# Seven block products for eight in 14 slabs of the down projections of a two-block transformer kernel

## The reference, cut to what matters

```python
def swiglu(x, w_gate, w_up, w_down):          # D_MODEL 1024, D_FF 2816
    return (jax.nn.silu(x @ w_gate) * (x @ w_up)) @ w_down

x = layer_norm(alpha * x + 0.5 * swiglu(...), ln_g[l, 0], ln_b[l, 0])        # first block
h = h + 0.5 * _swiglu(_rmsnorm(h, ffn_norm[layer, 0]), w_gate_up, w_down)    # second block
```

## Time and profile before

| what | value |
|---|---|
| median of 3 runs | 1599.74 us (1599.69 to 1599.82) |
| span of the profiled execution, first to last instruction | 1597.9 us |
| the profiled execution's own time | not listed apart from its span; the median of the runs is 1.8 us above the span |
| TensorE busy | 1591.1 us, 8788 matmuls |
| TensorE weight loads busy | 1369.5 us |
| VectorE busy | 1031.5 us, 1228 instructions |
| ScalarE busy | 801.4 us, 1092 instructions |
| DMA | 291.2 MB, 182 GB/s, 55.2% of the 16 engines |
| granted TensorE clock | 1.000 of full over the whole span |

### The profile page before, as it was taken

How to read it: one execution, slowest core, us unless ns; L and a number is a source line. 1 busy time by engine, 2 the same in 40 slices (tenths; PEclk the granted TensorE clock), 3 DMA queues, 4 the chain that set the end, 5 groups by cost and what they waited for, 6 DMA issues and landing times.

```text
span 1597.9 us, 21193 instructions
## 1 busy us (share of the span) xinstructions
PE 1591.1 (100%) x8788; PEld 1369.5 (86%) x8788; DVE 1031.5 (65%) x1228; ACT 801.4 (50%) x1092; POOL 35.5 (2%) x53
## 2 busy tenths in 40 slices
PE   9999999999999999999999999999999999999999
PEld 7888898878888888888899888889888888988887
DVE  6665656798766647665557666557766557766662
ACT  5555254775455525554344555446555436545550
POOL 0000000000000000000000000001000011000000
PEclk9999999999999999999999999999999999999999
DMA  9565574445567546665465655558565551056551
GB/s 308 187 218 184 171 260 154 141 139 181 170 196 231 199 163 199 194 200 186 157 224 176 194 185 203 197 171 254 175 189 199 187 198 56 28 174 192 187 186 77
DMA packets 226591, 291.21 MB, mean 182 GB/s; under 512 B 10628, under 2 KB 203840, under 8 KB 226368
## 3 DMA queue, kind: packets, MB, share of 16 engines
q1 hardware_dynamic: 226224, 289.61, 55.2%
q10 hardware_dynamic: 272, 0.26, 0.0%
HBM read 288.78 MB, written 1.05 MB: 181 GB/s over the span
## 4 chain that ended last, share of the span: by engine, by line
PE 95%; DVE 3%; ACT 1%; POOL 0%; issue 0%; DVEq 0%
PE bank L2089 24%; PE bank L2094 12%; PE bank L1878 9%; PE bank L1883 9%; PE bank L1887 9%; PE bank L1966 6%; PE bank L1958 6%; PE bank L1953 6%; PE bank L1927 2%; PE bank L1934 2%; PE bank L1929 2%; PE bank L2496 1%; PE bank L1854 1%; DVE w_lo L1160 1%; PE bank L2460 1%; PE bank L2471 1%
## 5 line engine op out<-in xcount | busy, mean ns | idle before, releaser
L1160 DVE TENSOR_TENSOR w_lo<-raw,w_hi 128x2048 fp32r<-128x2048 f32 (+1 forms) x267 | 599.3, 2269 | 166.8 <-ACT w_hi L729 164.5
L729 ACT ACTIVATE w_hi<-raw 128x2048 fp32r<-128x2048 f32 (+1 forms) x266 | 504.9, 1905 | 169.0 <-DMA raw<-in_ffn_w_down_dram 93.4
L2089 PE MATMUL bank<-xT,w_hi 128*128 128x512 f32 x1664 | 397.3, 391 | 0.0
L2089 PEld LDWEIGHTS bank<-xT,w_hi 128*128 128x128 f32 x1664 | 306.2, 188 | 59.5
L2094 PEld LDWEIGHTS bank<-xT,w_lo 128*128 128x128 f32 x1664 | 213.3, 191 | 8.1
L2094 PE MATMUL bank<-xT,w_lo 128*128 128x256 f32 x1664 | 215.9, 283 | 0.0
L1107 ACT ACTIVATE silu<-bank 128x256 f32<-128x256 f32 x104 | 34.2, 381 | 215.9 <-PE bank L2094 215.9
L1883 PE MATMUL bank<-w_hi,hT_lo 128*128 128x512 f32 x528 | 134.9, 390 | 0.0
L1878 PE MATMUL bank<-w_hi,hT_hi 128*128 128x512 f32 x528 | 133.8, 389 | 0.0
L1887 PE MATMUL bank<-w_lo,hT_hi 128*128 128x512 f32 x528 | 133.7, 389 | 0.0
L1953 PE MATMUL bank<-w_hi,xT 128*128 128x512 f32 (+2 forms) x448 | 117.6, 391 | 0.0
(11 more groups left out here) (294 smaller groups left out, 1572.4 us busy)
## 6 DMA issues: line engine op xcount, KB each, us to landing
raw<-in_ffn_w_gate_up_dram SPq DMA_DIRECT2D x176, 512.0 KB, 4.8
raw<-in_ffn_w_down_dram SPq DMA_DIRECT2D x132, 512.0 KB, 4.1
raw<-in_w_in_dram SPq DMA_DIRECT2D x44, 512.0 KB, 4.9
raw<-in_ffn_w_gate_dram SPq DMA_DIRECT2D x42, 512.0 KB, 4.0
raw<-in_ffn_w_up_dram SPq DMA_DIRECT2D x42, 512.0 KB, 5.0
raw<-in_conv_w_in_dram SPq DMA_DIRECT2D x24, 512.0 KB, 4.6
raw<-in_kv_w_dram SPq DMA_DIRECT2D x12, 512.0 KB, 4.4
raw<-in_w_out_dram SPq DMA_DIRECT2D x8, 512.0 KB, 3.9
```

What stands on the lines that cost most here:

```text
L729: nc.scalar.activation(w_hi[:, slot, 0:width], raw[:, slot, 0:width], ACT.Copy).then_inc(high_ready, 1)
L1160: nc.vector.tensor_tensor(w_lo[:, slot, 0:width], raw[:, slot, 0:width], w_hi[:, slot, 0:width].bitcast(F32), ALU.subtract).then_inc(low_r ...
L2089: nc.tensor.matmul(o[:], hi[:, c, at], x, start=kh == 0 and c == 0, stop=False, skip_group_check=True)
```

## The change

Three of the 11 down slabs (d = 3, 5, 7) in stages 0, 3, 5 and 9, and two (d = 3, 5) in stage 2, 14 in all, are multiplied by Strassen's method. The 2x2 blocks of the activations are (row block c of the slab) x (token tile); those of the weights are (row block) x (column half). The order of the down slabs becomes 0, 3, 1, 5, 2, 7, 4, 6, 8, 9, 10 (in stage 2: 0, 3, 1, 5, 2, 4, 6, 7, 8, 9, 10). Such a slab takes two slots: slot k has the loaded blocks, of which three are split; slot k + 1, for which nothing is loaded, gets four sums of blocks that VectorE makes in `raw`, and they are then split as any slab. VectorE also makes four sums of activation blocks in the tile after the silu. TensorE runs 9 matmuls on slot k and 12 on slot k + 1 in place of 24; four of the seven products go to banks 0, 1, 4 and 5, which the stage's last feature tile has used, and three straight to `Y`. Behind the last such slab ScalarE copies one bank out and VectorE adds the four shared products to the residual.

```diff
+SEVEN = {0: (3, 5, 7), 2: (3, 5), 3: (3, 5, 7), 5: (3, 5, 7), 9: (3, 5, 7)}
-    first_slab = [sum(LENGTH[k] for k in phases[:n]) for n in range(len(phases) + 1)]
+    first_slab = [sum(LENGTH[k] + len(SEVEN.get(m, ())) for m, k in enumerate(phases[:n])) for n in range(len(phases) + 1)]
...
+        P1, P5, P6, P7 = bank[0], bank[5], bank[1], bank[4]
...
+        def down_order(n):
+            plain = [d for d in range(FC // 2) if d not in sevens(n)]
+            order = []
+            for d in sevens(n):
+                order += [plain.pop(0), d]
+            return order + plain
...
+            if k in BLOCKS_OF:
+                return 3 * 512
...
+            def blocks(w, c0):
+                def pieces(slot):
+                    dst = raw[:, slot, :].rearrange("p (a n) -> p a n", a=4)
+                    return [(dst[:, 0:4:3, :], w[c0 * P:(c0 + 1) * P, :].rearrange("p (a n) -> p a n", a=2)),
+                            (raw[:, slot, 512:1536], w[(c0 + 1) * P:(c0 + 2) * P, :])]
+                return pieces
...
@@ ScalarE
-                act.wait_ge(arrived[slot], 32 * (k // SLOTS + 1))
+                if k in SUMS_OF:
+                    act.wait_ge(b_sums, SUMS_OF[k] + 1)
+                else:
+                    act.wait_ge(arrived[slot], 32 * loads_to(k))
...
+                        if j - 1 in sevens(n):
+                            i = sevens(n).index(j - 1)
+                            act.wait_ge(s_made, seven_before[n] + i + 1)
+                            nc.scalar.activation(s_hi[:, i], s_raw[:, i], ACT.Copy).then_inc(s_high, 1)
...
+                    if sevens(n):
+                        split_to(first_slab[n + 1] - 2)
+                        act.wait_ge(slab_used, last_seven(n))
+                        nc.scalar.activation(silu[:].rearrange("p a b -> p (a b)"), P1[:], ACT.Copy).then_inc(p1_copied, 1)
...
@@ VectorE
+            def block_sums(k):
+                b = raw[:, k % SLOTS, :].rearrange("p (a n) -> p a n", a=4)
+                made = raw[:, (k + 1) % SLOTS, :].rearrange("p (a n) -> p a n", a=4)
+                dve.wait_ge(arrived[k % SLOTS], 32 * loads_to(k))
+                dve.wait_ge(slab_used, k + 2 - SLOTS)
+                step(nc.vector.tensor_tensor(made[:, 0:2, :], b[:, 0:3:2, :], b[:, 3:4, :].to_broadcast([P, 2, 512]), ALU.subtract))
+                step(nc.vector.tensor_tensor(made[:, 2, :], b[:, 2, :], made[:, 0, :], ALU.add))
+                nc.vector.tensor_tensor(made[:, 3, :], b[:, 1, :], made[:, 2, :], ALU.subtract).then_inc(b_sums, 1)
...
+            def shared_products(n, factor):
+                w, p1 = h[:].rearrange("p a b -> p (a b)"), silu[:].rearrange("p a b -> p (a b)")
...
+                dve.wait_ge(p1_copied, ffn_seven[n] + 1)
+                step(nc.vector.tensor_tensor(w, P6[:], p1, ALU.add))
+                onto(first, P1[:])
+                onto(second, w)
+                step(nc.vector.tensor_tensor(p1, P7[:], w, ALU.add))
+                step(onto(rest, p1.unsqueeze(1).to_broadcast([P, 2, 512])))
+                nc.vector.scalar_tensor_tensor(out=right, in0=P5[:].unsqueeze(1).to_broadcast([P, 2, 512]), scalar=-1.0 if has_ln(n) else -factor,
+                                               in1=right, op0=ALU.mult, op1=ALU.add)
...
                         nc.vector.tensor_tensor(h[:], silu[:], h[:], ALU.mult).then_inc(h_ready, 2)
+                        if j in sevens(n):
+                            token_sums(j)
...
+                        if j - 1 in sevens(n):
+                            dve.wait_ge(s_high, seven_before[n] + i + 1)
+                            nc.vector.tensor_tensor(s_lo[:, i], s_raw[:, i], s_hi[:, i].bitcast(F32), ALU.subtract).then_inc(s_ready, 1)
...
+                    def token_sums(j):
+                        s, a = s_raw[:, sevens(n).index(j)], [[h[:, c, tt * P:(tt + 1) * P] for c in range(2)] for tt in range(NT)]
+                        dve.wait_ge(h_ready, 2 * FT * f + 2 * j + 2)
+                        nc.vector.tensor_tensor(s[:, 2, :], a[0][0], a[1][0], ALU.subtract)
+                        step(nc.vector.tensor_tensor(s[:, 0, :], a[1][0], a[1][1], ALU.add))
+                        step(nc.vector.tensor_tensor(s[:, 1, :], s[:, 0, :], a[0][0], ALU.subtract))
+                        nc.vector.tensor_tensor(s[:, 3, :], a[0][1], s[:, 1, :], ALU.subtract).then_inc(s_made, 1)
...
+                    if sevens(n):
+                        split_to(first_slab[n + 1] - 2)
+                        dve.wait_ge(slab_used, last_seven(n))
+                        shared_products(n, 0.5)
...
@@ TensorE
+                    def seven_products(k, d):
...
+                        own = [(P1, tokens(0, 0), 0), (Y[0][0], tokens(1, 0), 1), (Y[0][1], combined(3), 2)]
+                        made = [(P5, combined(0), 0), (P7, combined(2), 1), (P6, combined(1), 2), (Y[1][0], tokens(1, 1), 3)]
+                        pe.wait_ge(s_ready, seven_before[n] + i + 1)
+                        if i == 0:
+                            pe.wait_ge(up_joined, joined_before[n] + FT - token_tiles(n))
+                        for slab, group in ((k, own), (k + 1, made)):
+                            hi, lo = slab_view(slab % SLOTS, 4, 512)
+                            pe.wait_ge(high_ready, slab + 1)
+                            for o, (x_hi, _), at in group:
+                                nc.tensor.matmul(o[:], x_hi, hi[:, at, :], start=i == 0 and o in (P1, P5, P6, P7), stop=False, skip_group_check=True)
+                            for o, (_, x_lo), at in group:
+                                nc.tensor.matmul(o[:], x_lo, hi[:, at, :], start=False, stop=False, skip_group_check=True)
+                            pe.wait_ge(low_ready, slab + 1)
+                            for o, (x_hi, _), at in group:
+                                ins = nc.tensor.matmul(o[:], x_hi, lo[:, at, :], start=False, stop=d == sevens(n)[-1] and o in (P1, P5, P6, P7),
+                                                       skip_group_check=True)
+                            ins.then_inc(slab_used, 1)
```

More of the change, by code:

```diff
@@ L568, in _ @@
                     gains(n)
-                    for d in range(FC // 2):
-                        load(s0 + 2 * FT + d, rows(down, 2 * d))
+                    for i, d in enumerate(down_order(n)):
+                        load(down_slab(n, i), (blocks if d in sevens(n) else rows)(down, 2 * d))
                 elif kind == MIXER:
@@ L1201, in add_output, with onto @@
                 ins.then_inc(summed, 1)
+            def shared_products(n, factor):
+                w, p1 = h[:].rearrange("p a b -> p (a b)"), silu[:].rearrange("p a b -> p (a b)")
+                first, second, rest = x_sb[:, 0, 0:512], x_sb[:, 0, 512:D], x_sb[:, 1, :].rearrange("p (a n) -> p a n", a=2)
+                right = x_sb[:].rearrange("p t (a n) -> p t a n", a=2)[:, :, 1, :]
+                def onto(x, y):
+                    if has_ln(n):
+                        return nc.vector.scalar_tensor_tensor(out=x, in0=x, scalar=ALPHA / factor, in1=y, op0=ALU.mult, op1=ALU.add)
+                    return nc.vector.scalar_tensor_tensor(out=x, in0=y, scalar=factor, in1=x, op0=ALU.mult, op1=ALU.add)
+                dve.wait_ge(p1_copied, ffn_seven[n] + 1)
[6 more added lines that the diff above has]
+                                               in1=right, op0=ALU.mult, op1=ALU.add)
             def layer_norm(n, tt, factor):
@@ L1835, in _ @@
                         tile(j)
[L1836 to L1839, removed]
+                    if sevens(n):
+                        split_to(first_slab[n + 1] - 2)
+                        dve.wait_ge(slab_used, last_seven(n))
+                        shared_products(n, 0.5)
+                    split_to(first_slab[n + 1] + 3 - tail(n))
+                    boundary(n, 0.5, first_slab[n + 1])
         @block.tensor
@@ L1875, in part @@
                     if not known:
-                        pe.wait_ge(high_ready, s0 + d + 1)
+                        pe.wait_ge(high_ready, k + 1)
                     for c, toks, at, o in each:
-                        nc.tensor.matmul(o, lhs_hi[:, 2 * d + c, toks], hi[:, c, at], start=d == 0 and c == 0, stop=False,
+                        nc.tensor.matmul(o, lhs_hi[:, 2 * d + c, toks], hi[:, c, at], start=i == 0 and c == 0, stop=False,
                                          skip_group_check=True)
-                    for i, (c, toks, at, o) in enumerate(each):
-                        if between and i == len(each) // 2:
+                    for m, (c, toks, at, o) in enumerate(each):
+                        if between and m == len(each) // 2:
                             between()
@@ L1884, in part @@
                     if not known:
-                        pe.wait_ge(low_ready, s0 + d + 1)
+                        pe.wait_ge(low_ready, k + 1)
                     for c, toks, at, o in each:
```

(7 more changed lines are left out.)

49 lines of the change are left out of this document (41 added, 8 removed).

## The result

The kernel after takes **1591.09 us** (median of 4 runs, 1590.62 to 1591.44), the kernel before 1599.78 beside it (4 runs, 1599.69 to 1599.95). The ratio is 0.9946 [0.9934, 0.9957]: 8.7 us or 0.54% faster, where 9.5 were forecast. It lies inside the predicted range, 0.9 us above the predicted time.

A forecast was written before the change was run, and what follows sets the result against it. TensorE was taken to bound the kernel, matmul by matmul. Span 1597.9 less 9.52 us for 42 matmuls, added VectorE and ScalarE work costing 0, gives 1588.4; with 1.84 around it 1590.2 us, range 1589.3 to 1594.3.

The forecast's parts named there:

- TensorE sets the time: Down projections: 42 matmuls fewer at 226.7 ns take 9.52 us off, as long as the other engines keep up.
- the rival by which a matmul is worth 184 ns: Down projections: a removed matmul saves only its weight load's time, 7.7 us in all, 1592.0 us; chance 0.02.
- the one in which 21 take as long as 24: Rival, down slabs: matmuls spaced at 259 ns in place of 227, so no gain, 1599.7 us; chance 0.06.
- Cost of the sums: VectorE, each of 14 slabs: block sums 1.23 + 0.69 + 0.69 us, 2.66 with self-waits; upper end 5.3 us.
- partial cover: Rival: first pair and stage 0's boundary each late, 1 to 5 us given back, 1591.2 to 1595 us; chance 0.14.
- the overrun of VectorE: Rival, down stage: VectorE becomes the bound, slower from about 1.5 times the operations' cost, 1635 us at double; chance 0.06.
- First pair: First two slots, stage 0: joins end near 134.7, TensorE needs them at 137.1; cover 2.4 us, cost 0.
- Boundary of stage 0: End of stage 0's down projection: `y_ready` at 181.5, room for 2.5 to 4.3 us more VectorE work, cost 0.
- What is late first: If wrong: `y_ready` finds VectorE in its splits, and the transposes of the next stage's input wait.
- the price that the prediction put on doubled sums: First pair: joins end near 137.3, TensorE waits 0.2 to 1 us in each of five stages, 1 to 5 us.
- The high end of the range: 1594.3 us: most of the partial cover, up to doubled sums at the first pair in four or five stages.
- the allowance around the span: Whole kernel: 1.84 us between the profiled span and the median of the runs, added to the span of 1588.4.

The follow-up runs named there:

- Experiment 4: The kernel after with each seven-product down slab put ahead of the plain slab instead of behind it: 1607.62 us, ratio 1.005.
- experiment 3: The kernel after with each of the three block-sum operations run twice, same results: 1597.89 us, ratio 0.9989.

## Why the prediction was right

- *TensorE sets the time, and 42 matmuls are worth 227 ns each.* Shown. 9.50 us came out of the down projections against 9.52 counted; the rival by which a matmul is worth 184 ns (7.7 us) falls, and so does the one in which 21 take as long as 24. The Trainium skill's 131 ns for a matmul of 512 columns (TensorE: Matmul & The Clock Gate, Back-to-back issue gap) is in no run here; the pair of slots goes at 226.7 ns too.
- *Cost of the sums.* 1.22, 0.69 and 0.69 us, as plain operations of the width, so neither partial cover nor the overrun of VectorE came about. VectorE has 1138 us in place of 1147: rows back to back overlap by up to 0.08 us, which the sum counted twice, and the shared products took 5.1 us (166.35 to 171.48) for 5.5.
- *First pair.* Sums end at 128.5 for 129.0 forecast, the low part of slot k + 1 at 132.8 for 133.2, the joins at 134.1 for 134.7; cover 2.9 us for 2.4. Experiment 4 shows what the cover is worth.
- *Boundary of stage 0.* `y_ready` at 181.4 for 181.5 forecast, and 0.49 us of idle left ahead of it. The small margin was right.
- *What is late first.* Half right. The boundary was named; the low part of the third pair was not, and in experiment 3 it gives 4.5 us of wait. The step counted the work from 137.5 to `y_ready` as one sum and saw 3.1 us left, but each pair has a due time of its own. In the kernel after, the low part of slot k ends 4.5 us ahead of its due time at the second pair and 5.6 at the third; when every pair gets 2.66 us more, the third has to carry three of them and is the first to fail. So the price that the prediction put on doubled sums, a wait at the first pair and 1 to 5 us in all, was wrong in its place and its size: 0.17 us there in stage 0, and 6.9 in all. The high end of the range rests on that price, and the plain cost of the sums kept it from being tested by the result.
- *The 0.9 us that are missing.* The sum left out the mixer, 0.57 of span: 0.36 of it shown, by instructions that do nothing, to come from the place of instructions in VectorE's list. The step that failed is that a stage without an edit costs nothing. The other 0.2 is at the mixer's end, and it too comes only with seven products in stage 0. There ScalarE's copy starts 5.5 to 6.0 us behind the issue of its load in all nine traces of such kernels, and at most 5.1 in the five others; TensorE loses 0.15 to 0.4 us by it in seven of the nine and nothing in the others. Neither 40 nor 44 empty instructions bring it, so it isn't the place in the list; whether it is the shifted slots, no run separates. The rest of the 0.9 is the allowance around the span, 1.84 in the sum: the profiled execution, 1590.62 us, is itself 0.47 below the median, and the allowance was 1.72 for it and 2.19 for the median.

## What to carry to other kernels

Where TensorE's list is full, price the removed instructions by the start times of successive groups, not by their durations; and price the cover on the other engines at each due time, since one sum over the stage hides the one that fails first. An algebraic saving of 3 matmuls in 24 is bought with 6 us of VectorE here and stays only as long as every due time is met: 2.6 us more for each such slab takes it back. Compare landmarks in the stages that were not touched as well, and measure small effects against a variant in which only instructions that do nothing are added.

## What was not expected of the hardware

- A pause of 0.36 us between two VectorE instructions depends on where in the engine's list they stand: ahead of numbers 320 and 448, on three different instructions. The addition behind it has it as number 322, and not as 282, 326, 331 or 346. Adding 24 empty instructions made the kernel 0.3 to 0.5 us faster.
- After a wait of 2.13 us in a full stream TensorE's granted clock went to 0.50 for 3.4 us in four stages out of five, which nearly doubled the price of the wait; the runs of that kernel spread over 3.5 us, those of the others over 0.9 or less.
- The first 10 us differ by up to 0.7 us between executions of all these kernels, and that shift stays to the end: an effect under 1 us is to be read between landmarks, not from one span.
